# Sums of squares over four blocks on TensorE, one low half moved in the attention projections, two steps moved in the mLSTM layer

## What is computed

```python
for i in range(4):                       # mixers: mLSTM, windowed attention, neighbourhood attention, mLSTM
    mod = silu(cond) @ ada_w[i] + ada_b[i]               # shift, scale, gate for both halves of the layer
    h = rmsnorm(x, norm_w[i, 0]) * (1 + mod[1]) + mod[0]
    x = x + mod[2] * mixer(h)                            # attention: qkv, softmax, then @ w_o (1024 x 1024)
    h = rmsnorm(x, norm_w[i, 1]) * (1 + mod[4]) + mod[3]
    x = x + mod[5] * conv_ffn(h)                         # up 1024 -> 5632, conv of width 3, gate, down 2816 -> 1024
y = rmsnorm(x, final_norm_w)
# rmsnorm(x) = x * rsqrt(mean(x * x over the 1024 features) + eps) * w
```

## Time and profile before

| | us |
|---|---|
| median of 3 runs | 1842.92 (1841.68 to 1845.17) |
| the profiled execution's own time | 1840.74 |
| its span, first to last instruction | 1839.1 |
| TensorE busy (PE) | 1793.7 (98%) |
| VectorE busy (DVE) | 1389.5 (76%) |
| ScalarE busy (ACT) | 1002.4 (55%) |
| GpSimd busy (POOL) | 143.8 (8%) |
| mean granted TensorE clock | 0.996 |

### The profile page before, as it was taken

The page is one execution under the profiler, slowest core; times in us unless marked ns, Lnnn a source line. Parts: engine busy times, 40 slices in busy tenths (PEclk is TensorE's granted clock), DMA queues, the critical chain, the costliest instruction groups (busy, mean ns, idle before and its releaser), DMA issues.

```text
span 1839.1 us, 27506 instructions
## 1 busy us (share of the span) xinstructions
PE 1793.7 (98%) x11032; PEld 1494.3 (81%) x11032; DVE 1389.5 (76%) x2140; ACT 1002.4 (55%) x1567; POOL 143.8 (8%) x122
## 2 busy tenths in 40 slices
PE   5999999999999999999999999999999999999998
PEld 3988877797888867888977778888888787878888
DVE  3854777668898767999865698988665877779984
ACT  3744445446674454776354466745653445456753
POOL 1100121000000011000101100001100210010001
PEclk8999999999999999999999999999999999999999
DMA  9565656857665766675674777566555746445552
GB/s 393 211 225 197 203 207 242 307 221 292 261 216 205 288 250 265 252 277 198 216 311 166 298 283 294 204 224 266 207 185 183 240 163 225 171 172 195 197 173 80
DMA packets 74318, 421.27 MB, mean 229 GB/s; under 512 B 12400, under 2 KB 18952, under 8 KB 26576
## 3 DMA queue, kind: packets, MB, share of 16 engines
q1 hardware_dynamic: 56016, 395.68, 57.5%
q10 hardware_dynamic: 18176, 23.85, 4.0%
HBM read 408.51 MB, written 10.96 MB: 228 GB/s over the span
## 4 chain that ended last, share of the span: by engine, by line
PE 86%; DVE 5%; issue 3%; DMA 2%; ACT 2%; POOL 1%; SPq 0%; ACTq 0%; POOLq 0%; DVEq 0%
PE ps L654 17%; PE ps L676 10%; PE ps L711 9%; PE ps L657 9%; PE ps L636 6%; PE ps L692 5%; PE ps L714 5%; PE ps L639 3%; PE ps L622 3%; PE ps L624 3%; PE ps L623 3%; PE ps L755 3%; DMA raw<-in_stream 2%; DVE spl_lo L499 2%; PE ps L962 1%
## 5 line engine op out<-in xcount | busy, mean ns | idle before, releaser
L499 DVE TENSOR_TENSOR spl_lo<-raw,spl_hi 128x1024 fp32r<-128x1024 f32 x556 | 690.0, 1266 | 148.4 <-ACT spl_hi L488 147.1
L488 ACT ACTIVATE spl_hi<-raw 128x1024 fp32r<-128x1024 f32 x556 | 574.2, 1053 | 299.9 <-PE ps L714 109.5
L654 PE MATMUL ps<-H,spl_hi 128*128 128x512 f32 x1408 | 444.4, 397 | 3.7 <-DVE H L1854 2.9
L657 PEld LDWEIGHTS ps<-H,spl_lo 128*128 128x128 f32 x1408 | 264.5, 188 | 62.5
L657 PE MATMUL ps<-H,spl_lo 128*128 128x256 f32 x1408 | 276.7, 278 | 0.0
L654 PEld LDWEIGHTS ps<-H,spl_hi 128*128 128x128 f32 x1408 | 214.3, 189 | 17.9 <-issue 14.2
L711 PE MATMUL ps<-G,spl_hi 128*128 128x512 f32 x528 | 165.8, 395 | 0.0
L636 PE MATMUL ps<-B,spl_hi 128*128 128x512 f32 x512 | 160.8, 395 | 0.0
L622 PE MATMUL ps<-H,spl_hi 128*128 128x256 f32 x512 | 148.3, 290 | 1.8 <-DVE spl_lo L499 1.1
L623 PE MATMUL ps<-H,spl_hi 128*128 128x256 f32 x512 | 145.2, 284 | 0.0
L624 PE MATMUL ps<-H,spl_lo 128*128 128x256 f32 x512 | 145.0, 283 | 0.0
(11 more groups left out here) (251 smaller groups left out, 2927.4 us busy)
## 6 DMA issues: line engine op xcount, KB each, us to landing
raw<-in_stream SPq DMA_DIRECT2D x366, 1024.0 KB, 5.0
out_new_C<-c_stage ACTq DMA_DIRECT2D x16, 512.0 KB, 3.8
column<-in_ada_cols SPq DMA_DIRECT2D x16, 512.0 KB, 5.3
cond_all<-cond_out ACTq DMA_DIRECT2D x3, 1024.0 KB, 7.3
ada_b<-in_ada_b ACTq DMA_DIRECT2D x3, 768.0 KB, 9.1
E<-rows_out ACTq DMA_DIRECT2D x8, 256.0 KB, 4.3
Em<-rows_out ACTq DMA_DIRECT2D x8, 256.0 KB, 4.5
x<-in_x SPq DMA_DIRECT2D x1, 1024.0 KB, 6.7
```

The costliest lines, as they stand in the source:

```text
L488: act.activation(spl_hi[m % SPL][:, :], raw[r % RAW][:, h * HALF:(h + 1) * HALF], ACT.Copy).then_inc(S["hi_done"], 1)
L499: dve.tensor_tensor(spl_lo[m % SPL][:, :], raw[r % RAW][:, h * HALF:(h + 1) * HALF], spl_hi[m % SPL][:, :].bitcast(F32), ALU.subtract).the ...
L654: pe.matmul(banks[:, b * 512:(b + 1) * 512], spl_hi[m % SPL][:, c], H[:, kk * 512:(kk + 1) * 512], start=kk == 0, stop=False, skip_group_c ...
L657: mm = pe.matmul(banks[:, b * 512:b * 512 + TOK], spl_lo[m % SPL][:, c], H[:, kk * 512:kk * 512 + TOK], start=False, stop=kk == KD - 1, sk ...
```

## The change

square_sums multiplies all four blocks of sqa (two more matmuls in each of the nine norms), and GpSimd's third addition, the fold, goes. In the last step of the attention output projections the second low half of up 0 comes after the second half of the last residual and its scaling. After the last head of an mLSTM layer, gate_z(7) stands ahead of mod_rows. The fourth state copy of layer 3, with its two output issues, moves on ScalarE from the middle of norm 7 to the beginning of the last FFN, behind the high halves of up 1. The semaphore counts follow.

```diff
             def square_sums(q):
-                pe.wait_ge(S["sqa_done"], 3 * (q + 1))
-                for s in range(NS):
-                    pe.matmul(MISC[:, s:s + 1], sqa[:, s * T:(s + 1) * T], sc("ones"), start=s == 0, stop=False,
+                pe.wait_ge(S["sqa_done"], 2 * (q + 1))
+                for b in range(4):
+                    pe.matmul(MISC[:, b % NS:b % NS + 1], sqa[:, b * T:(b + 1) * T], sc("ones"), start=b == 0, stop=False,
                               skip_group_check=True)
...
                     head_rows(j, h)
                     if h == 0 and i == 0:
                         mod_rows(i, 1)
+                    if h:
+                        gate_z(2 * h + 1)
                     if h + 1 == MH:
                         mod_rows(i, 2)
-                    if h:
-                        gate_z(2 * h + 1)
...
             def square(q, pair):
-                if pair % 2 == 0 and 3 * q + pair > 0:
-                    act.wait_ge(S["sqa_done"], 3 * q + pair - 1)
+                if pair == 0 and q:
+                    act.wait_ge(S["sqa_done"], 2 * q)
                 elif pair == 1 and q:
                     act.wait_ge(S["ssq_mm"], q)
-                elif pair == 3:
-                    act.wait_ge(S["sqa_done"], 3 * q + 1)
+                elif pair >= 2:
+                    act.wait_ge(S["sqa_done"], 2 * q + 1)
...
-                    if late and g == 1:
-                        state(1, MH - 1, range(3, 4))
...
                 split_hi(act, n0 + 1)
+                if i + 1 == DEPTH:
+                    state(1, MH - 1, range(3, 4))
                 for j in range(NJ):
...
-                    split_lo(dve, n0 + t + 1)
+                    split_lo(dve, n0 + t + 1, (0,) if early else (0, 1))
...
                         residual(r, 3, 1)
                         scaled(3, r == 2 * DEPTH - 1)
+                        if early:
+                            split_lo(dve, n0 + t + 1, (1,))
...
             def square_total(q):
-                done = 3 * q
-                for k in range(3):
-                    pool.wait_ge(S["sq_done"], 5 * q + (2, 3, 3)[k])
-                    if k:
-                        pool.wait_ge(S["sqa_done"], done + k)
-                    elif q:
-                        pool.wait_ge(S["ssq_mm"], q)
-                    out, a, b = ((sqa[:, :], sq[0][:, :], sq[1][:, :]), (sqa[:, :], sqa[:, :], sq[0][:, :]),
-                                 (sqa[:, 0:TOK], sqa[:, 0:TOK], sqa[:, TOK:2 * TOK]))[k]
-                    pool.tensor_tensor(out, a, b, ALU.add).then_inc(S["sqa_done"], 1)
+                pool.wait_ge(S["sq_done"], 5 * q + 2)
+                if q:
+                    pool.wait_ge(S["ssq_mm"], q)
+                pool.tensor_tensor(sqa[:, :], sq[0][:, :], sq[1][:, :], ALU.add).then_inc(S["sqa_done"], 1)
+                pool.wait_ge(S["sq_done"], 5 * q + 3)
+                pool.wait_ge(S["sqa_done"], 2 * q + 1)
+                pool.tensor_tensor(sqa[:, :], sqa[:, :], sq[0][:, :], ALU.add).then_inc(S["sqa_done"], 1)
```

## The result

The changed kernel takes 1847.46 us (median of 12 runs, 1844.82 to 1853.67), the kernel before 1843.61 us in 12 runs beside it on the same chip (1840.39 to 1846.02). The ratio is 1.0020, 95% interval [1.0012, 1.0028]: slower, by 3.8 us where +2.3 was forecast (3.7 by the ratio, the figure used in the comparisons of the experiments). The profiled execution took 1847.34 us, 1845.7 of it span.

A forecast was written before the change was run, and what follows sets the result against it. TensorE, busy 1793.7 of 1839.1 us, was taken as the bound. The terms +2.8 + 1.6 - 1.2 - 0.9 = +2.3 us put the median 1842.92 at 1845.2 us, range 1840.5 to 1848.0.

The forecast's parts named there:

- part 2: Norms 3 and 5: second low half behind the last residual releases up 0 and a later load 0.8 late; +1.6 us.
- part 1: Sums of squares: two more matmuls without fold add 0.47 us in each of six norms; +2.8 us.
- both "late" rivals: ScalarE late in the last FFN (0.06), or up 1 late in both attention layers (0.07); each +3.8 us in all.
- The rival that TensorE loses this time anyway: Sums of squares: the two matmuls fit into time TensorE loses anyway; -0.5 us in all, chance 0.12.
- the release doesn't decide: Norms 3 and 5: the norm chain decides, the earlier residual brings 0.46 us each; -0.2 in all, chance 0.16.
- The 0.46 that I let the chain gain: Norms 3 and 5: the second half of the last squares starts 0.46 us earlier, so the chain to H gains that.
- allowed up 1 to take up the delay: Norm 3: if up 1 lands no later than before, the late release costs that norm nothing.
- The rule on shared access: Low halves: a two-input VectorE operation and a GpSimd operation exclude each other; first half ends at 720.9.
- Part 3: Layer 3: gate_z(7) before mod_rows removes TensorE's 1.16 us wait for copy_mod; -1.2 us.
- part 4: Norm 7: moving the fourth state copy out shortens TensorE's third wait for H from 1.08 to about 0.2; -0.9 us.
- the rival with ScalarE late: Last FFN: the moved copy and issues delay up 2's high half; +3.8 us in all, chance 0.06.
- Up 1 late in both layers: Both attention layers: up 1 also lands late over the ordered queue; +1.5 us on top, +3.8 in all, chance 0.07.

The follow-up runs named there:

- e9: The changed kernel with the second low half of up 0 back ahead of the last residual in norms 3 and 5; 1845.11 us, ratio 1.0004.
- e4: Kernel before plus moved gate_z(7) and state copy, and four blocks without fold in norms 3 and 5 only; 1839.14 us, ratio 0.9977.
- e2: Kernel before with only the second low half of up 0 moved behind the last residual and scaling, fold kept; 1846.02 us, ratio 1.0017.
- e6: The changed kernel with both low halves of up 0 behind the last residual in norms 3 and 5; 1850.49 us, ratio 1.0034.
- e11: The changed kernel once more, unchanged, for a second profile; 1849.07 us in this one run.
- e3: Kernel before with only the two moved steps, gate_z(7) before mod_rows and the fourth state copy in the last FFN; 1842.28 us, ratio 0.9990.
- e10: e2 with twelve extra matmuls in TensorE's wait for the raw tile in norms 3 and 5; 1852.24 us, ratio 1.0041.
- e12: The changed kernel with twelve extra matmuls in TensorE's wait for the raw tile in norms 3 and 5; 1851.92 us, ratio 1.0043.
- e7: e4 with the first ada tile ahead of up 0 in the load stream of norms 3 and 5; 1840.15 us, ratio 0.9978.
- e8: e7 with the second low half of up 0 behind the last residual; 1841.45 us, ratio 0.9987.

## Why the prediction was right, and where it was short

**The sum.** +2.3 forecast, +3.8 [+2.2, +5.2] measured: the mechanism forecast was the one that ran, and one term was too small. That the total came so near is in part luck: taken at their medians, part 2 was 1.5 over its price and part 1 was 0.6 under it. And the number alone doesn't choose: both "late" rivals stood at +3.8. It is the traces that rule them out.

**Part 1 (+2.8 forecast) stands.** 72 records, 0.91 us instead of 0.94 for a norm, the roots later by 0.44 to 0.45 for 0.47, no TensorE wait ended by it outside norms 3 and 5. Alone it measured +2.2. The rival that TensorE loses this time anyway (+0 for the six) is out: e9 differs from e4 by just these blocks in the seven other norms, and is 4.9 us slower (1.0004 against 0.9977), where 7 x 0.47 are 3.3. One effect I left out: without the fold, VectorE's halves no longer share with GpSimd's second addition. Both halves take 3.16 us in e9 and 3.69 before, so the fold's end by itself brings the release 0.5 us forward. Seen from e9, then, the moved half delays it by 1.3 us a norm: 2.5 of the 3.0 that it costs inside the change.

**Part 2 (+1.6 forecast) has the right mechanism and too small a price: +3.1 alone, 3.0 within the change.** The release of up 0 decided. SP issues 2.83 us behind the start of the last projection matmul (723.87 to 726.7) where it was 2.09 (720.51 to 722.6): +0.74 for the 0.8 forecast. The rival "the release doesn't decide" (-0.2 in all) is refuted by e2 and by the dose of e6. In norm 5 the bracket came out at 1.73, for the 1.7 forecast, and the norm became 0.8 longer, as forecast. In norm 3 it became 2.2 longer, and the profiled execution adds up to that: 0.7 for the later issue; 0.8 for the load, which took 5.6 us where I had carried over 4.8, and in e11 7.0; 1.5 for the lower clock; less 0.9, since TensorE no longer waits for up 1's low half. The lengths of landings scatter, and since TensorE now waits for this load in full, their scatter goes straight onto the path. The last term is the one by which I had allowed up 1 to take up the delay. The clock my rivals did not contain at all.

The price of the clock is read between the first matmul on H and the first on up 1, in norm 3 and then in norm 5 of the kernel after (columns as in the windows above):

```profile
733.36:741.76 8.40, 8.40 (x44) 6.22 (x41) 4.96 (x11) 3.69 (x7) 0.00 (x0) 0.80 1.01 425
1073.57:1080.45 6.88, 6.88 (x44) 5.20 (x41) 5.15 (x13) 4.04 (x9) 0.00 (x0) 1.00 1.01 427
```

TensorE runs the same 44 records without a pause in both, in 8.40 us with 3.4 us of half clock and in 6.88 without: 1.5 us. In e2 the two are 8.40 and 6.87. In norm 3 before, the same stretch took 7.8 us, its wait for up 1's low half included: that is the 0.9. The 0.46 that I let the chain gain was 0.52 (second half of the last squares 2.56 behind the projection, it was 3.08).

The rule on shared access that the prediction leaned on held: the half that lies beside a GpSimd addition took 2.03 and ended 1.1 us behind that addition (724.27 against 723.18); the moved one took 1.22. By the Trainium skill ("SBUF — State Buffer", "Who interferes with whom") this is the later operation blocked until the first is done; e9's 0.5 fits it.

On the clock, the traces show five falls at eight long waits. The Trainium skill, "TensorE: Matmul & The Clock Gate", section "HAM oscillation — how this bites in real kernels", says that a wait for data between groups of matmuls makes the next group start slow. The traces agree for those five, show three such waits without a fall (1.73, 1.74 and 2.27 us), and six falls for which this section has no wait to name.

**Part 3 (-1.2) and part 4 (-0.9) stand**: -1.8 measured for -2.1. The bracket of 1.16 is gone, and the third H wait is 0.19 for the 0.2 forecast. Norm 7 is 0.9 shorter in e3. No wait for spl_lo opens the last FFN's third tile: the rival with ScalarE late is out.

**"Up 1 late in both layers" (+1.5 on top) did not happen** as described: there is no bracket at up 1 in norms 3 and 5 of the kernel after. The delay is taken at the ada tile ahead of it, once.

**What stays open.** The split of norm 3 above is that of one execution; how often the others lose the clock there, and how long the load takes in them, their times don't tell. Nor is it shown that the long wait causes the fall of the clock. Five of eight against none of twenty speaks for it, and among the twenty are the four norms of e10 and e12 whose wait was filled; but these carry twelve more matmuls, and no run took the wait away and left all else. The profiled execution after is 6.6 us longer than that of before, more than the medians: in its first 45 us the clock was at the lower level for 13.7 us, 10.2 before, and norm 1 has a wait of 0.83 for a low half, 0.33 in e9. I take both for scatter, which is argued and not shown.

## What to carry to other kernels

Before moving an operation behind something on the critical chain, ask what it releases: here the low half was off the chain to H, but it freed the slot of the next load in an ordered queue, so the 0.5 us saved on that chain brought nothing, and the 0.7 by which the load came later went onto the path in each norm. Then price the new wait by the worst landing seen, not by the one in the profile, and ask what a fall of the clock would add: here it came with five of eight waits of 1.7 us or more, and a stretch of 3.4 us cost 1.5. And drop a fold only where an engine waits behind it: in two norms that gave 2.4 us, in all nine it cost 2.2.

## What the runs showed of the hardware

- Four float32 matmuls into four different 32-column strips run side by side: eight records of 512 columns take 1.06 us. Into one strip (e10), 24 records of 256 columns take 5.2 us, 0.22 each. A matmul that fills part of the array can't be priced from a group that fills it. The Trainium skill has the mechanism in "TensorE: Matmul & The Clock Gate", "Part 3: Packing small matmuls — row/col tiling"; the trace agrees.
- The load of one raw tile, the same tile at the same place of the program, took 4.7 to 7.0 us to land (before 4.8, e2 4.7, e9 4.8, after 5.6, e11 7.0).
- A stretch of 3.4 us at the lower clock cost 1.5 us where TensorE had work all through (44 records in 8.40 us against 6.88 in the kernel after), and 1.6 in e12.
- The granted clock fell in norm 5 of kernels in which TensorE stood still for nothing behind the projection (e7, e8, e12), and in norm 5 of e3 but not of the kernel before, which run the same code there.
